# Bias of both attentions: from stages of its own into the attention stages

## The chip, the cores and the metric

The kernel runs on one core of a Trainium2 chip. The metric is the device time of one execution in microseconds (us). Three runs of the kernel before gave 3819.38, 3820.43 and 3822.8 us, median 3820.43 us.

## The reference

The model is a trunk of two layers over 1024 tokens of width 1024, each a mixer and a SwiGLU block. Layer 0 mixes with a gated recurrence (HGRN2) and with an attention of 8 heads over three dilated patterns, (window, dilation) = (128, 1), (512, 4), (2048, 16), whose three softmaxes are joined by their log sums. Layer 1 (NSA) has 16 query heads on 4 key heads and adds three attentions: over compressed blocks, over selected blocks, and over a window of 512.

The kernel folds the parts of the score that depend on the distance d = query - key alone into an additive bias. In layer 0 a key within reach of n patterns has weight n: the bias is log(n), or -1e30 where n = 0 or d < 0. In layer 1 there are two masks, each 0 or -1e30: causal (d >= 0) and window (0 <= d < 512).

## The kernel before

The program is a sequence of stages. Each opens its semaphores and buffers, gives every engine a list of instructions, and closes with a clearing of its semaphores and a barrier over all engines; nothing of a stage starts before that barrier (class `Stage`, line 56). Matmuls are done in split fp32: an operand is cut into a high part (ScalarE, `ACT.Copy`) and a low part (VectorE, subtract).

A bias is a table of 128 partitions x 1024 distances. It is used in two shapes: `rows` (as made) for the maxima of a query block, and `cols` (each 128x128 block transposed) for the scores. Both are added by matmuls against an identity.

Layer 0, between the recurrence and the attention, has two stages:
- `dilated_bias_stage` (line 2119): GpSimd's iota makes the distances (L2136); VectorE makes the bias in 15 instructions over 128x1024, each waiting for the one before (L2144 to L2164); GpSimd's affine_select puts -1e30 where d < 0 (L2138).
- `bias_parts_stage` (line 1292): 8 transposes on TensorE (L1305), `rows` and `cols` high by ScalarE (L1309, L1311), `cols` low by VectorE (L1317).

Layer 1, between the selection and the attention, has three: `distance_bias_stage` (line 2168: a memset and two affine_selects on GpSimd, L2176 to L2181), and `bias_parts_stage` for the causal and for the window mask, without a low part.

`attention_stage` (line 1341) is called twice, as "at0" with 2 heads a round and as "at1" with 4; both have 4 rounds over loops written out by hand. Its beginning sets the order around the change:
- GpSimd makes `base` (L1515, L1517, L1520);
- ScalarE copies the identity, and from `base` fills parts of `ka` and `kc` (L1625, four times L1631); VectorE clears constants and `qa` (L1678 to L1682). These count `setup` up to 7;
- SyncE waits for `setup` 7 and issues the loads of queries, keys and values (L1483, L1493, L1496);
- TensorE waits for `setup` 7 and for the first loads, and does the maxima of the first unit (L1550), on which everything else of the stage depends. VectorE takes the maxima from PSUM (L1686), GpSimd builds `shift` (L1529), TensorE does the scores (L1570), ScalarE the exponentials into `pr` (L1637).
- In later rounds SyncE reloads a head's queries when the head's last values are done (`pv_done`, L1509), and TensorE waits for them.

Of the kernel before, what the change touches and what calls it, by code (L numbers as in the profile page):

```python
# [17 lines left out]
F32 = mybir.dt.float32  # L18
# [6 lines left out]
P = 128  # L25
# [1263 lines left out]
                    tokens(n)  # L1289


def bias_parts_stage(nc, name, bias, rows, cols, ident):


    with Stage(nc, name) as st:
        tr = st.ps("tr", [P, 2, BANK])
        tr_done, hi_done = st.sem("tr_done"), st.sem("hi_done")
        block = st.block()
        hi, lo = cols

        @block.tensor
        def _(pe):
            for d in range(TT):
                at = SEQ - (d + 1) * P
                nc.tensor.transpose(tr[:, d // 4, (d % 4) * P:(d % 4 + 1) * P], bias[:, at:at + P], ident[:]).then_inc(tr_done, 1)  # L1305

        @block.scalar
        def _(act):
            nc.scalar.activation(rows[:], bias[:], ACT.Copy)  # L1309
            act.wait_ge(tr_done, TT)  # L1310
            nc.scalar.activation(hi[:], tr[:, :, :].rearrange("p a b -> p (a b)"), ACT.Copy).then_inc(hi_done, 1)  # L1311

        @block.vector
        def _(dve):
            if lo is not None:
                dve.wait_ge(hi_done, 1)
                nc.vector.tensor_tensor(lo[:], tr[:, :, :].rearrange("p a b -> p (a b)"), hi[:].bitcast(F32), ALU.subtract)  # L1317


class Branch:  # L1320


# [18 lines left out]
def attention_stage(nc, name, n_heads, qT, branches, mixed, col0, ident, gates=None, selT=None):  # L1341
# [47 lines left out]
    with Stage(nc, name) as st:  # L1389
# [11 lines left out]
        rl = st.sb("rl", [P, U, S])  # L1401
        sc = st.sb("sc", [P, U, S])
        o_sb = st.sb("o", [P, S, HD])
        ps_m = st.ps("ps_m", [P, 2, BANK])
        ps_s = st.ps("ps_s", [P, RB, BANK])
        ps_o = st.ps("ps_o", [V1, 2, BANK])
# [1 line left out]
        q_in = [st.sem(f"q_in{h}") for h in range(H)]  # L1408
        k_in = [st.sem(f"k_in{s}") for s in range(SETS)]
        v_in = [st.sem(f"v_in{s}") for s in range(SETS)]  # L1410
        block_row, setup, m_done, piece_done, top_done, shift_done, s_done, p_done, hi_done, lo_done, pv_done, v_hi_done = (
            st.sem(n) for n in ("block_row", "setup", "m_done", "piece_done", "top_done", "shift_done", "s_done", "p_done", "hi_done",
                                "lo_done", "pv_done", "v_hi_done"))
# [3 lines left out]

        maxima_at = {step: [] for step in range(-C, C)}
        for u in range(U):
# [89 lines left out]
        @block.gpsimd  # L1512
        def _(pool):

            nc.gpsimd.memset(base[:], 1.0).then_inc(block_row, 1)  # L1515
            pool.wait_ge(block_row, 1)
            nc.gpsimd.affine_select(out=base[:], in_=base[:], compare_op=ALU.is_ge, fill=0.0, base=SLC * SEL0,  # L1517
                                    pattern=[[1, SEQ]], channel_multiplier=-SLC).then_inc(block_row, 1)
            pool.wait_ge(block_row, 2)
            nc.gpsimd.affine_select(out=base[:], in_=base[:], compare_op=ALU.is_ge, fill=0.0, base=SLC - 1 - SLC * SEL0,  # L1520
                                    pattern=[[-1, SEQ]], channel_multiplier=SLC).then_inc(block_row, 1)
            ident4 = ident[:].rearrange("p (o c) -> p o c", o=1).to_broadcast([P, S, P])

            with pool.Fori(0, ROUNDS) as it:
                for u in range(U):

                    pool.wait_ge(top_done, it * U + u + 1)
                    pool.nop(nofuse=True)
                    nc.gpsimd.tensor_tensor(shift[:, u % 2, :].rearrange("p (n c) -> p n c", c=P), ident4,  # L1529
                                            bcast(top[:, u, 0, :].rearrange("p (n o) -> p n o", o=1), P), ALU.mult)\  # L1530
                        .then_inc(shift_done, 1)

        @block.tensor
        def _(pe):
            pe.wait_ge(setup, 7)
            def maxima(it, m):
                u, x, j, w, _ = pieces[m]
                s, hh, br, strip = units[u]
# [85 lines left out]
        def _(act):  # L1624
# [27 lines left out]
            def split(it, s):  # L1652
                act.wait_ge(v_in[s], it * 16 + 16)
                nc.scalar.activation(v_hi[:, s, :, 0:HD], v_raw[:, s, :, :], ACT.Copy).then_inc(v_hi_done, 1)

            split(0, 0)
            for c in range(3):
                exps(0, c)
# [18 lines left out]
        def _(dve):  # L1677
# [2 lines left out]
                nc.vector.memset(to[:, :, :, HD:V1].bitcast(F32), value)  # L1680
            nc.vector.memset(qa[HD:P, :, :].bitcast(F32), 0.0).then_inc(setup, 1)
            nc.vector.memset(o_sb[:], 0.0).then_inc(o_free, 1)  # L1682
            def maximum(it, m):
                u, x, _, w, half = pieces[m]
                dve.wait_ge(m_done, it * M + m + 1)
                ins = nc.vector.tensor_reduce(top[:, u, half, x:x + 1], ps_m[:, m % 2, 0:w * P], AX.X, ALU.max)  # L1686
                ins.then_inc(piece_done, 1)
                if m == pieces_of[u][-1]:
                    dve.wait_ge(piece_done, it * M + m + 1)
                    ins = nc.vector.tensor_tensor(top[:, u, 0, :], top[:, u, 0, :], top[:, u, half, :], ALU.max)  # L1690
                    ins.then_inc(top_done, 1)
# [424 lines left out]
            output(TT - 1)  # L2116


def dilated_bias_stage(nc, bias):

    reach = ((128, 1), (512, 4), (2048, 16))
    with Stage(nc, "dil") as st:
        d = st.sb("d", [P, SEQ], I32)
        r = st.sb("r", [P, SEQ], I32)
        df = st.sb("df", [P, SEQ])
        a = st.sb("a", [P, SEQ])
        b = st.sb("b", [P, SEQ])
        c = st.sb("c", [P, SEQ])  # L2130
        step, iota_done = st.sem("step"), st.sem("iota_done")
        block = st.block()

        @block.gpsimd
        def _(pool):
            nc.gpsimd.iota(d[:], pattern=[[-1, SEQ]], base=SEQ - P, channel_multiplier=1).then_inc(iota_done, 1)  # L2136
            pool.wait_ge(step, 15)
            nc.gpsimd.affine_select(out=bias[:], in_=a[:], compare_op=ALU.is_ge, fill=NEG, base=SEQ - P,  # L2138
                                    pattern=[[-1, SEQ]], channel_multiplier=1)

        @block.vector
        def _(dve):
            dve.wait_ge(iota_done, 1)
            nc.vector.tensor_copy(df[:], d[:]).then_inc(step, 1)  # L2144
            dve.wait_ge(step, 1)
            nc.vector.tensor_scalar(c[:], df[:], float(reach[0][0]), None, ALU.is_le).then_inc(step, 1)
            for n, (window, dilation) in enumerate(reach[1:]):

                at = 2 + 4 * n
                nc.vector.tensor_scalar(r[:], d[:], dilation - 1, None, ALU.bitwise_and).then_inc(step, 1)  # L2150
                dve.wait_ge(step, at + 1)
                nc.vector.tensor_scalar(a[:], r[:], 0.0, None, ALU.is_equal).then_inc(step, 1)
                dve.wait_ge(step, at + 2)
                nc.vector.scalar_tensor_tensor(b[:], df[:], float(window), a[:], ALU.is_le, ALU.mult).then_inc(step, 1)
                dve.wait_ge(step, at + 3)
                nc.vector.tensor_tensor(c[:], c[:], b[:], ALU.add).then_inc(step, 1)
                dve.wait_ge(step, at + 4)

            nc.vector.tensor_scalar(a[:], c[:], 0.0, NEG, ALU.is_equal, ALU.mult).then_inc(step, 1)
            for n, count in enumerate((2, 3)):  # L2160
                at = 11 + 2 * n
                nc.vector.tensor_scalar(b[:], c[:], float(count), math.log(count), ALU.is_equal, ALU.mult).then_inc(step, 1)
                dve.wait_ge(step, at + 1)
                nc.vector.tensor_tensor(a[:], a[:], b[:], ALU.add).then_inc(step, 1)  # L2164
                dve.wait_ge(step, at + 2)


def distance_bias_stage(nc, causal, window):

    with Stage(nc, "dist") as st:  # L2170
        step = st.sem("step")
        block = st.block()

        @block.gpsimd
        def _(pool):
            nc.gpsimd.memset(causal[:], 0.0).then_inc(step, 1)  # L2176
            pool.wait_ge(step, 1)
            nc.gpsimd.affine_select(out=causal[:], in_=causal[:], compare_op=ALU.is_ge, fill=NEG, base=SEQ - P,
                                    pattern=[[-1, SEQ]], channel_multiplier=1).then_inc(step, 1)
            pool.wait_ge(step, 2)  # L2180
            nc.gpsimd.affine_select(out=window[:], in_=causal[:], compare_op=ALU.is_ge, fill=NEG, base=WIN - 1 - (SEQ - P),  # L2181
                                    pattern=[[1, SEQ]], channel_multiplier=-1)


def store_stage(nc, x_sb, out):
    with Stage(nc, "store") as st:
        x_out = st.sem("x_out")
# [8 lines left out]
def trunk(nc, x, attn_norm, ffn_norm, hy_w_in, hy_lb_logits, hy_o_gain, hy_q_gain, hy_k_gain, hy_w_out, nsa_w_in,  # L2196
# [22 lines left out]
    with ExitStack() as whole:  # L2219
        def sb(ctx, name, shape, dt=F32):  # L2220
            return ctx.enter_context(nc.sbuf_tensor(name, shape, dt))
# [26 lines left out]
        with ExitStack() as c:  # L2248
            mixed = sb(c, "mixed0", [P, TT, DM])
            hgrn_stage(nc, proj0, hy_lb_logits, mixed, ident)  # L2250
            with ExitStack() as c2:
                rows, cols = sb(c2, "dil_rows", [P, SEQ], F32R), parts(c2, "dil_cols", [P, SEQ])
                with ExitStack() as c3:
                    bias = sb(c3, "dil_bias", [P, SEQ])
                    dilated_bias_stage(nc, bias)
                    bias_parts_stage(nc, "dil_parts", bias, rows, cols, ident)
                at = 4 * A_WIDTH + 2 * B_HEADS * HD
                dilated = Branch(k0T, proj0[:, at:at + B_HEADS * HD], 1, rows, cols, range(TT), TT)
                attention_stage(nc, "at0", B_HEADS, q0T, [dilated], mixed, A_WIDTH, ident)
# [22 lines left out]
        with ExitStack() as c:  # L2282
            mixed = sb(c, "mixed1", [P, TT, DM])
            with ExitStack() as c2:
# [4 lines left out]
                masks = []  # L2289
                for mask in ("causal", "window"):  # L2290
                    masks.append((sb(c2, f"{mask}_rows", [P, SEQ], F32R), [sb(c2, f"{mask}_cols", [P, SEQ], F32R), None]))
                with ExitStack() as c3:
                    causal, window = sb(c3, "causal", [P, SEQ]), sb(c3, "window", [P, SEQ])
                    distance_bias_stage(nc, causal, window)
                    bias_parts_stage(nc, "causal_parts", causal, *masks[0], ident)
                    bias_parts_stage(nc, "window_parts", window, *masks[1], ident)
                vs, vw = DM + 3 * KV_W, DM + 5 * KV_W
                picked = Branch(some(k1T, 0), proj1[:, vs:vs + KV_W], GROUP, *masks[0], (0,), TT, C_HEADS, True)
                near = Branch(some(k1T, 4), proj1[:, vw:vw + KV_W], GROUP, *masks[1], (0, WIN // P), WIN // P + 1, 2 * C_HEADS)
# [27 lines left out]
```

## Time and profile before

| | |
|---|---|
| median of 3 runs | 3820.43 us |
| the profiled execution, its own time | 3820.43 us |
| its span, first to last instruction | 3818.7 us |
| TensorE busy | 3304.1 us (87%) |
| VectorE, ScalarE, GpSimd busy | 43%, 32%, 4% |
| mean granted TensorE clock | 0.926 |

The profile is one execution. A busy share is a mean over stages; the change touches two short stretches between long stages, so what counts is how long each stretch is and which instruction ends it. PE is TensorE, PEld its weight load, DVE VectorE, ACT ScalarE, POOL GpSimd, SP SyncE; a q behind the name is the engine's queue. PEclk 1.00 is 2.4 GHz, 0.50 is 1.2 GHz.

### The profile page before, as it was taken

Reading aid. Unit: us, or ns where it says so; the run is one execution under the profiler, and the core shown is the slowest. Engines: PE = TensorE matmul, PEld = TensorE weight load, DVE = VectorE, ACT = ScalarE, POOL = GpSimd, SP = SyncE. Lnnn points to the kernel's source line nnn. Section 1 sums busy time; section 2 is a strip of 40 time slices with the busy share of each in tenths; the row PEclk is TensorE's granted clock in tenths of the full one; section 3 lists DMA queues with packets and bytes.
Section 4 is the critical chain, followed back from the end, with each engine's and each line's share of the span. In section 5 each row is a group of like instructions: output and inputs, shape, how many; then the busy total and the mean of one; then the engine's idle time right before and its main releaser. Section 6 shows DMA issues by size and latency. Waiting matters only on the chain. (4 is left out here: it accounts for less than half of the span.)

```text
span 3818.7 us, 44633 instructions
## 1 busy us (share of the span) xinstructions
PE 3304.1 (87%) x16522; PEld 2764.2 (72%) x16522; DVE 1623.4 (43%) x2983; ACT 1204.1 (32%) x2469; POOL 149.1 (4%) x189
## 2 busy tenths in 40 slices
PE   5999575578779999999799755999998889999998
PEld 4887465466658888888588654877877768888887
DVE  3132776445332323232442054887887133232323
ACT  3122332334122112212332153665665122121211
POOL 0000000000000000000000121111110000000000
PEclk9999687789889999999899676999999989999999
DMA  3334100332111212121273513113111022212212
GB/s 119 97 101 105 38 19 23 68 68 45 47 44 54 79 45 83 55 72 50 64 171 93 102 37 68 33 34 67 34 33 35 16 61 64 67 61 69 69 53 88
DMA packets 264014, 241.70 MB, mean 63 GB/s; under 512 B 41944, under 2 KB 203736, under 8 KB 263800
## 3 DMA queue, kind: packets, MB, share of 16 engines
q1 hardware_dynamic: 263800, 238.86, 23.7%
q8 instruction: 133, 2.18, 0.2%
q14 instruction: 81, 0.66, 0.1%
HBM read 193.52 MB, written 45.29 MB: 63 GB/s over the span
## 5 line engine op out<-in xcount | busy, mean ns | idle before, releaser
L498 PE MATMUL ffn_acc<-ffn_hT_hi,ffn_w_hi 128*128 128x512 f32 x1408 | 435.8, 391 | 17.8 <-DVE ffn_w_lo L579 17.8
L498 PE MATMUL ffn_acc<-ffn_hT_lo,ffn_w_hi 128*128 128x512 f32 x1408 | 435.4, 391 | 0.0
L498 PE MATMUL ffn_acc<-ffn_hT_hi,ffn_w_lo 128*128 128x512 f32 x1408 | 435.2, 390 | 0.0
L579 DVE TENSOR_TENSOR ffn_w_lo<-ffn_raw,ffn_w_hi 128x1024 fp32r<-128x1024 f32 x88 | 107.8, 1225 | 738.8 <-ACT ffn_w_hi L538 738.8
L1153 PE MATMUL in_acc<-in_w_hi,hT_hi 128*128 128x512 f32 (+1 forms) x832 | 330.4, 397 | 15.2 <-DVE in_w_lo L1233 15.2
L538 ACT ACTIVATE ffn_w_hi<-ffn_raw 128x1024 fp32r<-128x1024 f32 x88 | 93.3, 1060 | 750.4 <-PE ffn_acc L498 737.4
L1637 ACT ACTIVATE at_pr<-at_ps_s 128x512 f32<-128x512 f32 x480 | 223.8, 466 | 332.6 <-PE at_ps_s L1570 330.1
L1155 PE MATMUL in_acc<-in_w_hi,hT_lo 128*128 128x512 f32 (+1 forms) x832 | 325.1, 391 | 0.0
L1154 PE MATMUL in_acc<-in_w_lo,hT_hi 128*128 128x512 f32 (+1 forms) x832 | 324.7, 390 | 0.0
L1696 DVE TENSOR_TENSOR at_p_lo<-at_pr,at_p_hi 128x512 fp32r<-128x512 f32 x480 | 272.6, 585 | 108.9 <-ACT at_p_hi L1644 108.5
L498 PEld LDWEIGHTS ffn_acc<-ffn_hT_hi,ffn_w_hi 128*128 128x128 f32 x1408 | 265.5, 189 | 73.4 <-DVE ffn_w_lo L579 18.3
L498 PEld LDWEIGHTS ffn_acc<-ffn_hT_lo,ffn_w_hi 128*128 128x128 f32 x1408 | 265.5, 189 | 55.3
L498 PEld LDWEIGHTS ffn_acc<-ffn_hT_hi,ffn_w_lo 128*128 128x128 f32 x1408 | 265.5, 189 | 55.3
L1686 DVE TENSOR_REDUCE at_top<-at_ps_m 128x1 f32<-128x512 f32 (+1 forms) x480 | 243.4, 525 | 128.4 <-PE at_ps_m L1550 125.7
L518 PE MATMUL ffn_acc_d<-ffn_d_hi,ffn_a_hi 128*128 128x512 f32 x704 | 274.0, 389 | 0.0
L520 PE MATMUL ffn_acc_d<-ffn_d_hi,ffn_a_lo 128*128 128x512 f32 x704 | 274.0, 389 | 0.0
L519 PE MATMUL ffn_acc_d<-ffn_d_lo,ffn_a_hi 128*128 128x512 f32 x704 | 274.0, 389 | 0.0
L1550 PE MATMUL at_ps_m<-at_kc,at_qa 128*128 128x512 f32 (+1 forms) x480 | 177.2, 382 | 106.6 <-DMA at_qb<-q0T_lo 36.5
L1644 ACT ACTIVATE at_p_hi<-at_pr 128x512 fp32r<-128x512 f32 x480 | 237.9, 497 | 0.0
L1153 PEld LDWEIGHTS in_acc<-in_w_hi,hT_hi 128*128 128x128 f32 x832 | 165.1, 198 | 46.4 <-DVE in_w_lo L1233 17.5
L549 ACT ACTIVATE ffn_d_hi<-ffn_d_raw 128x512 fp32r<-128x512 f32 x176 | 108.3, 629 | 277.9 <-PE ffn_acc_d L520 277.9
L1550 PEld LDWEIGHTS at_ps_m<-at_kc,at_qa 128*128 128x128 f32 x480 | 95.1, 198 | 138.2 <-issue 78.5
(310 smaller groups left out, 5779.3 us busy)
## 6 DMA issues: line engine op xcount, KB each, us to landing
ffn_d_raw<-in_ffn_w_down SPq DMA_DIRECT2D x176, 256.0 KB, 3.0
ffn_raw<-in_ffn_w_gate SPq DMA_DIRECT2D x44, 512.0 KB
ffn_raw<-in_ffn_w_up SPq DMA_DIRECT2D x44, 512.0 KB
in_raw<-in_hy_w_in SPq DMA_DIRECT2D x56, 256.0 KB
proj<-in_nat SPq DMA_DIRECT2D x40, 256.0 KB, 2.1
in_raw<-in_nsa_w_in SPq DMA_DIRECT2D x40, 256.0 KB
at_qa<-q1T_hi SPq DMA_DIRECT2D x16, 264.0 KB
x_sb<-in_x SPq DMA_DIRECT2D x1, 4096.0 KB
```

The lines of the kernel that those rows point to most:

```text
L498: ins = nc.tensor.matmul(acc[:, m, half, :], w[:, m, k, :], h[:, k, half * HALF:(half + 1) * HALF], start=k == 0 and w is w_hi and h is hT ...
L518: nc.tensor.matmul(acc_d[:, x, :], a_hi[:, k, rows], d_hi[:, n % R, :], start=k == 0, stop=False)
L519: nc.tensor.matmul(acc_d[:, x, :], a_hi[:, k, rows], d_lo[:, n % R, :], start=False, stop=False)
L520: ins = nc.tensor.matmul(acc_d[:, x, :], a_lo[:, k, rows], d_hi[:, n % R, :], start=False, stop=k == G - 1)
L1153: nc.tensor.matmul(acc[:, n % 4, 0:cols], x_hi, r_hi, start=k == 0, stop=False)
L1154: nc.tensor.matmul(acc[:, n % 4, 0:cols], x_hi, r_lo, start=False, stop=False)
L1155: ins = nc.tensor.matmul(acc[:, n % 4, 0:cols], x_lo, r_hi, start=False, stop=k == KD - 1)
L1550: ins = nc.tensor.matmul(ps_m[:, m % 2, pos * P:(pos + n) * P], lhsT, rhs, start=x == 0, stop=x == len(parts) - 1, skip_group_check=True)
L1637: nc.scalar.activation(pr[:, c % R, 0:w], ps_s[:, c % RB, 0:w], ACT.Exp).then_inc(p_done, 1)
L1644: nc.scalar.activation(p_hi[:, c % R, 0:w], pr[:, c % R, 0:w], ACT.Copy).then_inc(hi_done, 1)
L1686: ins = nc.vector.tensor_reduce(top[:, u, half, x:x + 1], ps_m[:, m % 2, 0:w * P], AX.X, ALU.max)
L1696: nc.vector.tensor_tensor(p_lo[:, c % R, 0:w], pr[:, c % R, 0:w], p_hi[:, c % R, 0:w].bitcast(F32), ALU.subtract).then_inc(lo_done, 1)
```

## The change

The five stages go. What they did stands at the beginning of `attention_stage`. The table being made lies in `pr` (`temp(n)`, two of its six buffers each), the transposes go to banks of `ps_s` and `ps_m`; only the dilated chain has a new buffer, `more`, of 3 x 1024 a partition. GpSimd does its part behind `base`, VectorE its 15 instructions behind its memsets, ScalarE its copies behind the four L1631 and ahead of the first values' split. TensorE does the transposes ahead of its wait for `setup`, and begins the maxima only when the `cols` are done.

```diff
-def bias_parts_stage(nc, name, bias, rows, cols, ident):
...
@@ attention_stage
+        dilated = gates is None
+        more = st.sb("more", [P, 3, SEQ]) if dilated else None
...
+        def temp(n):
+            return pr[:, 2 * n:2 * n + 2, :].rearrange("p a b -> p (a b)")
+
+        bias_tr_of = [ps_s[:, 0:2, :].rearrange("p a b -> p (a b)"), ps_m[:].rearrange("p a b -> p (a b)")]
+        NBIAS = 1 if dilated else 2
...
@@ gpsimd, behind base
+            if dilated:
+                nc.gpsimd.iota(temp(1).bitcast(I32), pattern=[[-1, SEQ]], base=SEQ - P, channel_multiplier=1).then_inc(iota_done, 1)
+                pool.wait_ge(bias_step, 15)
+                nc.gpsimd.affine_select(out=temp(0), in_=more[:, 0, :], compare_op=ALU.is_ge, fill=NEG, base=SEQ - P,
+                                        pattern=[[-1, SEQ]], channel_multiplier=1).then_inc(bias_done, 1)
+            else:
+                nc.gpsimd.memset(temp(0), 0.0).then_inc(bias_step, 1)
+                pool.wait_ge(bias_step, 1)
+                nc.gpsimd.affine_select(out=temp(0), in_=temp(0), compare_op=ALU.is_ge, fill=NEG, base=SEQ - P,
+                                        pattern=[[-1, SEQ]], channel_multiplier=1).then_inc(bias_done, 1)
+                pool.wait_ge(bias_done, 1)
+                nc.gpsimd.affine_select(out=temp(1), in_=temp(0), compare_op=ALU.is_ge, fill=NEG, base=WIN - 1 - (SEQ - P),
+                                        pattern=[[1, SEQ]], channel_multiplier=-1).then_inc(bias_done, 1)
...
@@ tensor
+            for n in range(NBIAS):
+                pe.wait_ge(bias_done, n + 1)
+                for d in range(TT):
+                    at = SEQ - (d + 1) * P
+                    ins = nc.tensor.transpose(bias_tr_of[n][:, d * P:(d + 1) * P], temp(n)[:, at:at + P], ident[:])
+                ins.then_inc(bias_tr, 1)
             pe.wait_ge(setup, 7)
+            pe.wait_ge(cols_done, NBIAS)
...
@@ scalar, behind setup
+            for n in range(NBIAS):
+                act.wait_ge(bias_done, n + 1)
+                nc.scalar.activation(branches[n].rows[:], temp(n), ACT.Copy)
+                act.wait_ge(bias_tr, n + 1)
+                nc.scalar.activation(branches[n].cols[0][:], bias_tr_of[n], ACT.Copy).then_inc(cols_hi if dilated else cols_done, 1)
             split(0, 0)
...
@@ vector, behind the memsets; the 15 instructions of dilated_bias_stage, in buffers of pr and more
+            if dilated:
+                d, df, a, b, c, r = (temp(1).bitcast(I32), temp(2), more[:, 0, :], more[:, 1, :], more[:, 2, :], more[:, 1, :].bitcast(I32))
+                dve.wait_ge(iota_done, 1)
...
+                dve.wait_ge(cols_hi, 1)
+                nc.vector.tensor_tensor(branches[0].cols[1][:], bias_tr_of[0], branches[0].cols[0][:].bitcast(F32), ALU.subtract)\
+                    .then_inc(cols_done, 1)
...
@@ trunk
-                with ExitStack() as c3:
-                    bias = sb(c3, "dil_bias", [P, SEQ])
-                    dilated_bias_stage(nc, bias)
-                    bias_parts_stage(nc, "dil_parts", bias, rows, cols, ident)
...
-                    distance_bias_stage(nc, causal, window)
-                    bias_parts_stage(nc, "causal_parts", causal, *masks[0], ident)
-                    bias_parts_stage(nc, "window_parts", window, *masks[1], ident)
```

## Rows read from the trace of the kernel before

**Rows 1.** Page, part 1: busy us (share) xinstructions.

```profile
PE 3304.1 (87%) x16522; PEld 2764.2 (72%) x16522; DVE 1623.4 (43%) x2983; ACT 1204.1 (32%) x2469; POOL 149.1 (4%) x189
```

**Rows 2.** Windows view of the stretches: from:to, length, busy by engine.

```profile
core 0: us, PE busy (x) PEld busy (x) DVE busy (x) ACT busy (x) POOL busy (x), PEclk, DMA share, GB/s
664.03:685.70 21.67, 1.94 (x8) 1.57 (x8) 14.63 (x16) 2.08 (x2) 2.02 (x3) 0.50 0.00 0
685.70:707.11 21.41, 0.00 (x0) 0.00 (x0) 2.27 (x5) 4.20 (x5) 3.03 (x3) 0.50 0.65 113
707.11:716.30 9.19, 8.85 (x24) 6.33 (x24) 4.13 (x9) 2.51 (x3) 1.04 (x1) 0.50 0.94 163
2315.38:2327.03 11.65, 3.88 (x16) 3.14 (x16) 0.00 (x0) 4.16 (x4) 3.02 (x3) 0.50 0.00 0
2327.03:2349.18 22.15, 0.00 (x0) 0.00 (x0) 3.97 (x5) 4.20 (x5) 3.03 (x3) 0.50 0.66 114
...
707.11:960.00 252.89, 199.07 (x1024) 160.45 (x1024) 124.26 (x248) 99.79 (x217) 20.12 (x17) 0.90 0.30 60
2349.18:2930.00 580.82, 554.49 (x3581) 467.19 (x3582) 474.28 (x1092) 351.57 (x840) 72.29 (x64) 0.99 0.19 39
```

**Rows 3.** Timeline, layer 0's two bias stages: start, length, what, [idle before].

```profile
658.90 4.42 DVE L1032 TENSOR_TENSOR mixed<-mixed,hgo_sg 128x4096 f32<-128x4096 f32 x1
664.03 0.98 POOL L2136 IOTA dil_d<- 128x1024 int32 x1 [281.29 <-ACTq L67]
665.05 0.69 DVE L2144 CAST dil_df<-dil_d 128x1024 f32<-128x1024 int32 x1 [1.72 <-POOL dil_d L2136]
...
677.64 1.23 DVE L2164 TENSOR_TENSOR dil_a<-dil_a,dil_b 128x1024 f32<-128x1024 f32 x1
679.01 1.04 POOL L2138 TENSOR_SCALAR_AFFINE_SELECT dil_bias<-dil_a 128x1024 f32<-128x1024 f32 x1 [14.00 <-DVE dil_a L2164]
...
680.76 1.06 ACT L1309 ACTIVATE dil_rows<-dil_bias 128x1024 fp32r<-128x1024 f32 x1 [29.53 <-PEq L70]
680.79 1.94 PE L1305 MATMUL dil_parts_tr<-ident,dil_bias 128*128 128x128 f32 x8 [43.31 <-PEq L70]
682.76 1.02 ACT L1311 ACTIVATE dil_cols_hi<-dil_parts_tr 128x1024 fp32r<-128x1024 f32 x1 [0.94 <-PE dil_parts_tr L1305]
683.82 1.22 DVE L1317 TENSOR_TENSOR dil_cols_lo<-dil_parts_tr,dil_cols_hi 128x1024 fp32r<-128x1024 f32 x1 [4.95 <-ACT dil_cols_hi L1311]
```

**Rows 4.** Timeline, the beginning of at0.

```profile
685.70 0.95 POOL L1515 MEMSET at_base<- 128x1024 f32 x1 [5.65 <-POOLq L70]
...
686.72 1.04 POOL L1517 TENSOR_SCALAR_AFFINE_SELECT at_base<-at_base 128x1024 f32<-128x1024 f32 x1
687.83 1.04 POOL L1520 TENSOR_SCALAR_AFFINE_SELECT at_base<-at_base 128x1024 f32<-128x1024 f32 x1
688.38 0.27 DVE L1682 MEMSET at_o<- 128x256 f32 x1
...
691.75 1.04 ACT L1631 ACTIVATE at_kc<-at_base 64x1024 fp32r<-64x1024 f32 x1
692.81 0.38 SPq L1483 DMA_DIRECT2D at_qa<-q0T_hi  x1
...
707.14 0.45 PE L1550 MATMUL at_ps_m<-at_kc,at_qa 128*128 128x128 f32 x1 [24.42 <-DMA at_kb<-k0T_hi]
```

**Rows 5.** Timeline, layer 1: the mask stages and the beginning of at1.

```profile
2315.38 0.95 POOL L2176 MEMSET causal<- 128x1024 f32 x1 [41.12 <-POOLq L70]
...
2333.08 1.04 ACT L1631 ACTIVATE at_kc<-at_base 64x1024 fp32r<-64x1024 f32 x1
...
2349.22 0.45 PE L1550 MATMUL at_ps_m<-at_kc,at_qa 128*128 128x128 f32 x1 [24.14 <-DMA at_kb<-k1T_hi]
```

**Rows 6.** Waits view of 707 to 1010 us: us in total, times, longest.

```profile
PE at_ps_m L1550 <- DMA at_qb<-q0T_lo: 36.5, 6, 6.8
```

**Rows 7.** Page, part 5: a VectorE instruction that runs while weights stream in.

```profile
L579 DVE TENSOR_TENSOR ffn_w_lo<-ffn_raw,ffn_w_hi 128x1024 fp32r<-128x1024 f32 x88 | 107.8, 1225 | 738.8 <-ACT ffn_w_hi L538 738.8
```

More of the change, by code:

```diff
@@ L1289, in _ @@
                     tokens(n)
-def bias_parts_stage(nc, name, bias, rows, cols, ident):
[L1295 to L1317, printed above, removed]
 class Branch:
@@ L1410, in attention_stage @@
         v_in = [st.sem(f"v_in{s}") for s in range(SETS)]
+        bias_step, bias_done, bias_tr, cols_hi, cols_done, iota_done = (
+            st.sem(n) for n in ("bias_step", "bias_done", "bias_tr", "cols_hi", "cols_done", "iota_done"))
         block_row, setup, m_done, piece_done, top_done, shift_done, s_done, p_done, hi_done, lo_done, pv_done, v_hi_done = (
@@ L1415, in attention_stage @@
         block = st.block()
+        def temp(n):
+            return pr[:, 2 * n:2 * n + 2, :].rearrange("p a b -> p (a b)")
+        bias_tr_of = [ps_s[:, 0:2, :].rearrange("p a b -> p (a b)"), ps_m[:].rearrange("p a b -> p (a b)")]
+        NBIAS = 1 if dilated else 2
+        reach = ((128, 1), (512, 4), (2048, 16))
         maxima_at = {step: [] for step in range(-C, C)}
@@ L1682, in _ @@
             nc.vector.memset(o_sb[:], 0.0).then_inc(o_free, 1)
+            if dilated:
+                d, df, a, b, c, r = (temp(1).bitcast(I32), temp(2), more[:, 0, :], more[:, 1, :], more[:, 2, :], more[:, 1, :].bitcast(I32))
+                dve.wait_ge(iota_done, 1)
+                nc.vector.tensor_copy(df, d).then_inc(bias_step, 1)
+                dve.wait_ge(bias_step, 1)
+                nc.vector.tensor_scalar(c, df, float(reach[0][0]), None, ALU.is_le).then_inc(bias_step, 1)
+                for n, (reached, dilation) in enumerate(reach[1:]):
+                    at = 2 + 4 * n
+                    nc.vector.tensor_scalar(r, d, dilation - 1, None, ALU.bitwise_and).then_inc(bias_step, 1)
+                    dve.wait_ge(bias_step, at + 1)
+                    nc.vector.tensor_scalar(a, r, 0.0, None, ALU.is_equal).then_inc(bias_step, 1)
+                    dve.wait_ge(bias_step, at + 2)
+                    nc.vector.scalar_tensor_tensor(b, df, float(reached), a, ALU.is_le, ALU.mult).then_inc(bias_step, 1)
+                    dve.wait_ge(bias_step, at + 3)
+                    nc.vector.tensor_tensor(c, c, b, ALU.add).then_inc(bias_step, 1)
+                    dve.wait_ge(bias_step, at + 4)
+                nc.vector.tensor_scalar(a, c, 0.0, NEG, ALU.is_equal, ALU.mult).then_inc(bias_step, 1)
+                for n, count in enumerate((2, 3)):
+                    at = 11 + 2 * n
+                    nc.vector.tensor_scalar(b, c, float(count), math.log(count), ALU.is_equal, ALU.mult).then_inc(bias_step, 1)
+                    dve.wait_ge(bias_step, at + 1)
+                    nc.vector.tensor_tensor(a, a, b, ALU.add).then_inc(bias_step, 1)
+                    dve.wait_ge(bias_step, at + 2)
+                dve.wait_ge(cols_hi, 1)
+                nc.vector.tensor_tensor(branches[0].cols[1][:], bias_tr_of[0], branches[0].cols[0][:].bitcast(F32), ALU.subtract)\
+                    .then_inc(cols_done, 1)
             def maximum(it, m):
@@ L2116, in _ @@
             output(TT - 1)
[L2119 to L2165, printed above, removed]
@@ L2168, in distance_bias_stage @@
[L2168 to L2182, printed above, removed]
@@ L2291, in trunk @@
                     masks.append((sb(c2, f"{mask}_rows", [P, SEQ], F32R), [sb(c2, f"{mask}_cols", [P, SEQ], F32R), None]))
-                with ExitStack() as c3:
-                    causal, window = sb(c3, "causal", [P, SEQ]), sb(c3, "window", [P, SEQ])
-                    distance_bias_stage(nc, causal, window)
-                    bias_parts_stage(nc, "causal_parts", causal, *masks[0], ident)
-                    bias_parts_stage(nc, "window_parts", window, *masks[1], ident)
                 vs, vw = DM + 3 * KV_W, DM + 5 * KV_W
```

## The prediction

> **What bounds the kernel now.** The page's first part says that TensorE is busy for 87% of the span [rows 1]. That share says little here: the change lies in the other 13%. So I read windows next, one for each stretch between the last work of the stage ahead and the first maxima of the attention. There are four of them, and in all four TensorE stands nearly still. The two bias stages of layer 0 take 21.67 us, with 14.63 us of VectorE as the longest term; the three of layer 1 take 11.65 us; the beginnings of at0 and at1 take 21.41 and 22.15 us, with no TensorE work, 2.3 to 4.2 us on each other engine and a DMA share of 0.65 [rows 2]. The timeline says what ends each: in the bias stages, the chain of instructions itself and the barriers; in the beginnings, the loads. TensorE's first maxima come at 707.14 and at 2349.22 us and both were released by the DMA of `kb` [rows 4, 5]. The reader is to see two serial pieces, one made of engine work and one made of transfers, on disjoint resources: in the bias stages the DMA share is 0.00.
>
> **What is removed.** The stretches 664.03 to 685.70 and 2315.38 to 2327.03, barriers included: 21.67 + 11.65 = 33.32 us [rows 2]. Both begin with the first instruction behind the barrier of the stage ahead (the last VectorE work there ends at 658.90 + 4.42 = 663.32, 0.71 us earlier) [rows 3], and end with the first instruction of the attention stage, so the attention stage will begin where they began. Its own 0.7 us of barrier stays.
>
> **What the beginning of at0 becomes.** I count from its first instruction, T0 (685.70 before).
> - Loads: GpSimd's `base` ends at 687.83 + 1.04 = T0 + 3.17; ScalarE's last fill at 691.75 + 1.04 = T0 + 7.09; the first load is issued at T0 + 7.11 [rows 4]. The diff puts nothing ahead of any of them: GpSimd's new work is behind `base`, ScalarE's behind the fills, VectorE's behind the memset that counts for `setup`, and nothing is added on SyncE. The loads land as before, and TensorE could start at 707.14 - 685.70 = T0 + 21.44.
> - The bias chain, link by link: iota behind `base`, with the 0.07 us gap between instructions of GpSimd [rows 4] and 0.98 us: T0 + 4.22. VectorE has by then ended its memsets (688.38 + 0.27 = T0 + 2.95) [rows 4] and starts 0.04 us later; its 15 instructions took from 665.05 to 677.64 + 1.23 = 678.87, 13.82 us: T0 + 18.08. The select starts 0.14 us later and takes 1.04: T0 + 19.26. Transposes, 0.07 + 1.94: T0 + 21.27. The high part, 0.03 + 1.02: T0 + 22.32. The low part, 0.04 + 1.22: T0 + 23.58. TensorE's wait, 0.07 [rows 3].
> - So TensorE starts at T0 + 23.65 instead of T0 + 21.44: the wait for `cols_done` now ends last, not the loads. The slip is 2.2 us.
>
> What is queued behind that wait is all of TensorE's list, and through it VectorE's maxima, GpSimd's `shift` and the exponentials. Does the slip reach the end of the stage? The other head's loads are in by then either way, and would hide it if TensorE met them late; but the waits for loads that follow (six, 36.5 us in all) [rows 6] are for reloads that SyncE issues only when TensorE has finished a head. They move with TensorE and absorb nothing. I take the slip in full; its ends are 0 and 7 us (the rivals below). Gain of layer 0: 21.67 - 2.2 = 19.5 us.
>
> **What the beginning of at1 becomes.** No VectorE chain here. GpSimd: `base` to T0 + 3.17 as in at0, then a memset and two selects, 0.95 + 1.04 + 1.04 with gaps of at most 0.14: T0 + 6.6. ScalarE is free at 2333.08 + 1.04 = 2334.12, T0 + 7.09 (T0 = 2327.03) [rows 2, 5], and then has two copies of 1.06 and two of 1.02 us [rows 3]: T0 + 11.3. The 16 transposes, from T0 + 5.5 on, lie beside it. TensorE can't start before the loads, at 2349.22 = T0 + 22.19 [rows 5], so 10.9 us of cover stay. The masks cost nothing and the gain is all of 11.65 us. If the cover were gone, it would cost what goes beyond those 10.9 us.
>
> **Costed at nothing.** The instructions in their new place beside loads: a VectorE instruction of 128x1024 with two inputs takes 1.225 us where weights stream in [rows 7], and 1.22 us in the bias stage with no DMA at all [rows 3]; so loads don't stretch it. Six more semaphores to clear at each end of attention, and the buffer `more`: no row prices them; the barrier with all around it is 0.71 us [rows 3], so I bound them by 0 and 0.7 us a stage and take 0, since they add no instruction to a chain.
>
> **The clock.** The clock was at 0.50 over the bias stages and the beginnings, and for 9.19 us after the first maxima of at0, in which TensorE was busy for 8.85 us [rows 2]. Now 1.94 us of transposes end 2.4 us before the first maxima; before, 24 us before. If they brought the rise forward by their own length and the gap, 4.3 us of the 9.19 would run at the double clock, and where TensorE's own work bounds them that gives back up to 4.3 / 2 = 2.2 us. I take 0, because eight transposes alone left the clock at 0.50 in both bias stretches. The Trainium skill, TensorE: Matmul & The Clock Gate, "The HAM clock gate", says that the half rate is the default and activity releases it, by which the result would be about 2 us lower, 3787; its part "PE-mode transpose" says that transposes don't count as such activity, by which it stays at 3789.
>
> **Sum.** 19.5 + 11.65 = 31.1 us. The profiled execution took 3820.43 us over a span of 3818.7, and equals the median of the runs. Predicted: 3820.43 - 31.1 = 3789.3 us.
>
> **The rivals.**
> - *The slip isn't passed on* (an earlier rise of the clock as above, or something later in the round that is late anyway). For it: nearly all of the 9.19 us is TensorE work at the low clock [rows 2]. Against it: the reloads follow TensorE [rows 6]. Gain 33.3 us: 3787.1 us.
> - *The chain is longer in its new place.* Nine of its 15 instructions have one input and take 0.69 us, six have two and take 1.22 [rows 3]; if the nine lost what makes them short (buffers cut out of `pr` and `more`, ScalarE's fills and the loads beside them), each would cost 0.53 more, 4.8 us, all of it on the path: a slip of 7 us, 3794.1 us. Against it: loads don't stretch the two-input kind [rows 7], and every buffer is still 1024 adjacent elements.
> - *The gaps that are removed come back elsewhere* (the attention stage needs time of its own to get going, which the bias stages had covered, so that the loads' issue comes later than T0 + 7.11). Were it so in both layers by as much as the barrier gap is long, 0.7 us each, nothing is seen; to cancel the gain to within 0.2% it would need 23 of 31 us. No row shows such a cost. About 3815 us.
> - *Slower: the clock.* The two attentions run at 0.90 and 0.99 from the first maxima on [rows 2], that is about 50 and 12 us at the low level. At that level a stretch bound by TensorE takes twice its time. If the new phase of the six reload waits and of the start made the clock rise later each time, this would have to add more than 62 us at the low level to lose 31 us: from there on the kernel is slower. With a doubling of both, and then some 16 us more beyond the level where it breaks even, the time is 3828 us. Against it: the waits stay as long as they were and TensorE's lists are the same.
>
> **How the numbers follow.** Forecast 0.76, its own range 3787 to 3792; not passed on 0.10; longer chain 0.09; gaps back 0.02; clock 0.01; the last 0.02 for a case I don't see, shared between no change and slower. The range reaches to the first two rivals and takes in 0.7 us a stage of the unpriced clearing, plus 1.7 us, half the spread of the runs before: 3785 to 3796. A measurement of this kernel tells some 0.2% (7.6 us) from no change. Faster by more: 0.76 + 0.10 + 0.09 = 0.95; within: 0.03; slower: 0.02.
>
> **What would show it.** In the profile after: at0's first GpSimd memset at 664.0 and its first load 7.1 us later; VectorE's chain 13.8 us long; the first maxima at 664.0 + 23.65 = 687.7, with ScalarE's or VectorE's `cols` as the releaser of TensorE's wait instead of `kb`. For at1: T0 at 2295.9, `cols` done at T0 + 11.3, first maxima at T0 + 22.2 = 2318.1, released by the DMA as before. The stretch from the first maxima of at0 to T0 of at1 (2315.38 - 707.14 = 1608.2 us) is unchanged. Wrong would be: loads issued later than T0 + 7.2; a chain over 14.5 us; a first maximum of at1 that waits for `cols_done`; or a changed length between the maxima of at0 and those of at1 by more than 2 us, which would mean that clock or slip work on later.

## The result and the profile after

| | before | after |
|---|---|---|
| median of 6 runs each | 3820.75 us | 3792.38 us |
| lowest to highest | 3816.77 to 3826.38 | 3788.32 to 3794.28 |
| profiled execution, its own time / span | 3820.43 / 3818.7 us | 3790.27 / 3788.6 us |
| mean granted clock | 0.926 | 0.932 |

The ratio is 0.9923 (95% interval 0.991 to 0.9936): 28.4 us less by the medians, 24 to 34 by the interval. The forecast was 31.1 us less, 3789.3 us; the interval holds it.

The windows of the kernel after, as in [rows 2]: the beginning of at0, the time at the low clock after its first maxima, at0's body (first maxima to last values), and the beginning of at1.

```profile
661.15:684.82 23.67, 1.97 (x9) 1.60 (x9) 16.91 (x21) 7.32 (x9) 5.01 (x5) 0.50 0.69 118
684.82:693.19 8.37, 8.07 (x22) 5.89 (x23) 3.71 (x8) 1.14 (x2) 1.04 (x1) 0.50 0.87 167
684.82:933.95 249.13, 201.20 (x1019) 162.09 (x1020) 123.97 (x246) 98.15 (x215) 19.16 (x16) 0.89 0.29 58
2295.70:2316.87 21.17, 3.54 (x17) 3.31 (x17) 3.98 (x5) 8.02 (x9) 6.00 (x6) 0.58 0.64 112
```

The reader is to see that VectorE's chain of 14.6 us and the loads (DMA share 0.69) now lie in one stretch of 23.67 us, where there were two, of 21.67 and 21.41 us [rows 2]. The timeline gives the links of the chain, to be laid beside [rows 3, 4]:

```profile
661.15 0.95 POOL L1498 MEMSET at_base<- 128x1024 f32 x1 [278.14 <-POOLq L70]
...
664.28 0.98 POOL L1506 IOTA at_pr<- 128x1024 int32 x1
665.29 0.69 DVE L1695 CAST at_pr<-at_pr 128x1024 f32<-128x1024 int32 x1 [1.20 <-POOL at_pr L1506]
...
668.26 0.38 SPq L1466 DMA_DIRECT2D at_qa<-q0T_hi  x1
...
677.89 1.23 DVE L1713 TENSOR_TENSOR at_more<-at_more 128x1024 f32<-128x1024 f32 x1
679.26 1.04 POOL L1508 TENSOR_SCALAR_AFFINE_SELECT at_pr<-at_more 128x1024 f32<-128x1024 f32 x1 [14.01 <-DVE at_more L1713]
680.34 1.06 ACT L1662 ACTIVATE dil_rows<-at_pr 128x1024 fp32r<-128x1024 f32 x1 [12.10 <-POOL at_pr L1508]
680.36 1.97 PE L1535 MATMUL at_ps_s<-ident,at_pr 128*128 128x128 f32 x8 [45.79 <-POOL at_pr L1508]
682.36 1.02 ACT L1664 ACTIVATE dil_cols_hi<-at_ps_s 128x1024 fp32r<-128x1024 f32 x1 [0.97 <-PE at_ps_s L1535]
683.49 1.22 DVE L1716 TENSOR_TENSOR dil_cols_lo<-at_ps_s,dil_cols_hi 128x1024 fp32r<-128x1024 f32 x1 [4.38 <-ACT dil_cols_hi L1664]
...
684.82 0.45 PE L1554 MATMUL at_ps_m<-at_kc,at_qa 128*128 128x128 f32 x1 [2.49 <-issue]
```

The low part ends at 684.71 and the first maxima start at 684.82; the row no longer names the DMA. In e1, where the beginning of at0 is the same, the row names the low part:

```profile
688.89 0.44 PE L1654 MATMUL at_ps_m<-at_kc,at_qa 128*128 128x128 f32 x1 [2.50 <-DVE dil_cols_lo L1816]
```

at1's first maxima are still released by the DMA, 10.2 us behind the end of the last `cols` (2305.62 + 1.01 = 2306.63):

```profile
2305.62 1.01 ACT L1664 ACTIVATE window_cols<-at_ps_m 128x1024 fp32r<-128x1024 f32 x1
...
2316.87 0.44 PE L1554 MATMUL at_ps_m<-at_kc,at_qa 128*128 128x128 f32 x1 [12.32 <-DMA at_kb<-k1T_hi]
```

Where the 30.1 us between the two spans lie (four of the six stretches aren't changed):

| stretch | before | after | difference |
|---|---|---|---|
| start to the first instruction behind the recurrence | 664.03 | 661.15 | -2.9 |
| from there to at0's first maxima | 43.11 | 23.67 | -19.4 |
| at0's body | 246.87 | 249.13 | +2.3 |
| its end to the first instruction behind the selection | 1361.37 | 1361.75 | +0.4 |
| from there to at1's first maxima | 33.84 | 21.17 | -12.7 |
| to the end | 1469.5 | 1471.7 | +2.2 |

The -2.9 us come ahead of anything that the change touches, and they are luck: over the kernels of this document this stretch takes 661.2 to 665.2 us. In the two profiles here the clock goes with it: over 382 to 433 us, in the recurrence, it is at 0.50 in the profile before and rises 6 us earlier in the one after:

```profile
382.00:433.00 51.00, 13.22 (x60) 12.45 (x61) 36.16 (x50) 17.72 (x15) 0.75 (x3) 0.50 0.24 63
```

```profile
382.00:433.00 51.00, 12.86 (x82) 11.90 (x83) 37.19 (x53) 17.72 (x15) 1.01 (x4) 0.56 0.25 64
```

### The profile page after: what moved, and what is told of

It reads as the page before. It is cut to its first block and busy times, and to the rows that moved or that the text cites. A ratio compares the mean times of both kernels' runs of the same rounds, so it can differ in the third digit from the quotient of the medians.

```text
span 3788.6 us, 44515 instructions
## 1 busy us (share of the span) xinstructions
PE 3305.4 (87%) x16522; PEld 2764.5 (73%) x16522; DVE 1624.0 (43%) x2983; ACT 1204.2 (32%) x2469; POOL 148.6 (4%) x189
## 5 line engine op out<-in xcount | busy, mean ns | idle before, releaser
L1155 PEld LDWEIGHTS in_acc<-in_w_hi,hT_lo 128*128 128x128 f32 x832 | 165.0, 198 | 31.1
```

What stands on the lines that cost most here:

```text
L1155: ins = nc.tensor.matmul(acc[:, n % 4, 0:cols], x_lo, r_hi, start=False, stop=k == KD - 1)
```

## The experiments

Every kernel but e12 was built from the kernel after by the edit shown. Ratios are taken against runs of the kernel before on the same chip (medians 3819.1 us beside e1 to e4, 3820.7 beside e5 to e8, 3820.0 beside e9 to e11). Where a time is compared with the kernel after (3792.38 us), the two weren't run beside each other, and from chip to chip the kernel before alone differs by 1.6 us; four or five runs of one kernel spread over 3 to 9 us. Such differences are good to some 3 us.

**e1: only layer 0.** `attention_stage` skips its own making in at1, and `trunk` calls the old stages there.

> Only layer 0's bias is made inside its attention stage; layer 1 keeps its three stages. Theory (the removed stretch less a slip of 2.2 us at the first maxima, rest unchanged): 19.5 us under before, some 3801 us; at0's first maxima at T0 + 23.65, at1's at T0 + 22.2 or, as in the changed kernel, 21.2. Rival (nothing of the slip is passed on): 21.7 us under before. Second rival (gains of the two layers are not additive, one of them covers the other): well off 19.5.

3802.52 us, ratio 0.9954 (0.9937 to 0.997): 17 us less, interval 11 to 24. First maxima at T0 + 23.68. The interval holds both 19.5 and 21.7, so it doesn't decide between theory and rival (e3 does); the profile places the slip where theory has it. at0's body was 250.1 us.

**e2: only layer 1.** The reverse.

> Only layer 1's masks are made inside its attention stage; layer 0 keeps its two stages. Theory (the removed stretch in full, all new work under the loads): 11.7 us under before, 12.7 if the loads land 1 us earlier after T0 as in the changed kernel; at1's first maxima released by the DMA of kb at T0 + 21.2 to 22.2. Rival (the gain of the changed kernel comes from layer 0 alone): no change.

3808.99 us, ratio 0.9973 (0.9964 to 0.9983): 10 us less, interval 6 to 14. at1's first maxima at T0 + 21.3, released by the DMA. The rival falls. The two parts add to 27 us, against 28 for the whole.

**e3: a longer chain in at0.**

```diff
+                for n in range(8):
+                    nc.vector.tensor_tensor(c, c, c, ALU.max).then_inc(chain_more, 1)
+                    dve.wait_ge(chain_more, n + 1)
                 nc.vector.tensor_scalar(a, c, 0.0, NEG, ALU.is_equal, ALU.mult).then_inc(bias_step, 1)
```

> The changed kernel with eight more VectorE instructions of 128x1024 in at0's bias chain (a maximum of c with itself, 1.22 us and a gap of 0.04 each). Theory (the chain ends last and its length goes to the end of the kernel one to one): 8 x 1.26 = 10.1 us over the changed kernel, first maxima at T0 + 33.8. Rival (the slip is taken up by something later in the first round, the reloads or the clock): under 6 us.

3802.14 us, 9.8 us over the changed kernel, for 10.1 us of chain; first maxima at T0 + 33.75. The body behind them takes 249.1 us, as in the kernel after, so nothing there took the delay up: what the chain adds goes to the end.

**e4: a longer mask in at1.**

```diff
                 pool.wait_ge(bias_done, 1)
+                for n in range(20):
+                    nc.gpsimd.affine_select(out=temp(1), in_=temp(0), ...).then_inc(chain_more, 1)
+                    pool.wait_ge(chain_more, n + 1)
```

> The changed kernel with twenty more affine_selects of 128x1024 ahead of the window mask in at1 (1.04 us and a gap of 0.14 each, 23.6 us). Theory (masks have 9.9 us of cover under the loads, from cols done at T0 + 11.3 to the first maxima at T0 + 21.2): the window mask comes at T0 + 30, cols at T0 + 33.2, first maxima there too and released by cols_done: 12 us over the changed kernel, not 23.6. Rival (masks were on the path already): 23.6 us over it. Second rival (other work than the loads covers more): under 8 us.

3803.86 us, 11.5 us over the changed kernel, for 23.5 us of selects. Timeline of at1's beginning (T0 = 2298.86):

```profile
2298.86 0.95 POOL L1499 MEMSET at_base<- 128x1024 f32 x1 [41.48 <-POOLq L70]
...
2304.25 23.49 POOL L1518 TENSOR_SCALAR_AFFINE_SELECT at_pr<-at_pr 128x1024 f32<-128x1024 f32 x20
...
2330.99 1.02 ACT L1669 ACTIVATE window_cols<-at_ps_m 128x1024 fp32r<-128x1024 f32 x1 [0.97 <-PE at_ps_m L1540]
...
2332.11 0.45 PE L1559 MATMUL at_ps_m<-at_kc,at_qa 128*128 128x128 f32 x1 [1.16 <-issue]
```

First maxima at T0 + 33.25, right behind the `cols`, and 12.1 us later than in the kernel after. Of the 23.6 us that the selects put in front of the window mask, 10.2 went into the cover under the loads (10.9 were worked out, 9.9 expected here), and 1.4 into the time in which ScalarE had been busy with other copies; the rest was paid. So the masks are made under the loads, and the cover is about as large as worked out.

**e5 and e6: the chain of at0 by one instruction shorter or longer.**

```diff
-                    nc.vector.scalar_tensor_tensor(b, df, float(reached), a, ALU.is_le, ALU.mult).then_inc(bias_step, 1)
+                    if reached < SEQ: (the line above) else: nc.vector.nop(nofuse=True).then_inc(bias_step, 1)
...
-                    nc.vector.tensor_tensor(c, c, b, ALU.add).then_inc(bias_step, 1)
+                    nc.vector.tensor_tensor(c, c, b if reached < SEQ else a, ALU.add).then_inc(bias_step, 1)
```

e6 adds one of e3's eight instructions.

> The changed kernel without the reach test of the third pattern in at0's chain (2048 reaches every distance, the bias is the same): 1.22 us and its gap less. Theory (the chain ends last, and the TensorE clock's level after each wait for loads hangs on where the waits fall): first maxima at T0 + 22.4; the clock is low for 9.6 us after them, as in the kernel before, and low for 3 to 4 us, not 5 to 6, after the first reload; at0's body, first maxima to last values, back from 249.1 to 250.1 us to the 245 to 247 us it had with the bias outside; 2 to 4 us under the changed kernel. Rival (only the chain counts): body 249 us and 1.3 us under the changed kernel.

> The changed kernel with one more VectorE instruction (maximum of c with itself) in at0's chain, 1.26 us. Theory of the clock: first maxima at T0 + 24.9, low clock for some 7.1 us after them instead of 8.4, and 3.6 to 4.4 us after the first reload instead of 4.9 to 5.7, body shorter by 1 us or more; the kernel as fast as the changed one or faster in spite of the longer chain. Rival: body unchanged and 1.3 us over the changed kernel.

3792.35 and 3792.67 us, with the changed kernel at 3792.38. First maxima at T0 + 22.52 and T0 + 24.92. The clock was low for 9.6 us after the first maxima in e5, as said; in e6 it rose after 3.7 us, not 7.1. After the first reload it was low for 6.2 us in e5 (3 to 4 expected) and 5.4 in e6 (3.6 to 4.4 expected). The bodies were 248.4 and 249.4 us: shorter than 249.1 to 250.1 by at most 1.7 us, not back at 245 to 247. As I had put it, my theory of the body fails. A chain of 1.2 us more or less can't be told in the total either, so neither rival (1.3 us less, 1.3 us more) is settled by the times.

**What the body is made of.** So I took the body apart in every profile: the gaps of TensorE at the six reloads (over 4 us from one matmul's start to the next's; in e9 and e11, described below, the matmuls thrown away don't count), the time outside them at a granted clock of 0.50, and the rest. Half of the low time is what it would cost if TensorE alone bounded it.

| profile | body | gaps | low clock | body - gaps - low/2 |
|---|---|---|---|---|
| before | 246.9 | 37.8 | 34.4 | 191.9 |
| before, once more (e12) | 244.1 | 35.1 | 32.2 | 192.8 |
| e2 (layer 0 as before) | 244.9 | 35.5 | 35.1 | 191.8 |
| after | 249.1 | 37.2 | 40.1 | 191.9 |
| e1 | 250.1 | 38.4 | 39.7 | 191.9 |
| e3 | 249.1 | 38.2 | 37.8 | 192.0 |
| e4 | 249.0 | 37.9 | 38.1 | 192.1 |
| e5 | 248.4 | 38.3 | 36.8 | 191.7 |
| e6 | 249.4 | 40.1 | 33.2 | 192.7 |
| e7 | 252.6 | 40.8 | 39.8 | 191.9 |
| e8 | 248.0 | 37.8 | 37.0 | 191.7 |
| e10 | 247.3 | 38.4 | 30.9 | 193.5 |
| e9 (reload fill) | 234.2 | 36.7 | 8.5 | 193.3 |
| e11 (reload fill) | 236.2 | 39.8 | 3.4 | 194.6 |

The last column lies within 1.1 us (191.7 to 192.8) wherever the low time is 32 us or more: the body holds no new work (1019 matmuls before and after), it differs by waits for reloads and by clock. With less low time the column rises, to 194.6 us in e11: half of the low time overstates what the clock costs, by up to 3 us of 18 here. And with the bias outside the body is 244.1 to 246.9 us in three profiles, with the bias inside and the reloads unfilled 247.3 to 252.6 in nine.

**e7, e8, e10: idle time of TensorE ahead of the first maxima filled.** e7 and e10 with transposes, e8 with fp32r matmuls of 128 columns:

```diff
+            def filler(n):
+                for _ in range(n):
+                    nc.tensor.transpose(ps_t[:, 0, 384:512], ident[:], ident[:])
+            if dilated:
+                pe.wait_ge(setup, 7)
+                filler(45)
             for n in range(NBIAS):
...
             pe.wait_ge(setup, 7)
+            filler(8 if dilated else 48)
```

> The changed kernel with idle time of TensorE ahead of the first maxima filled with transposes of the identity into unused columns of ps_t: in at0 45 ahead of the bias and 8 behind it, in at1 48 behind the bias (0.246 us each at the low clock, from the bias transposes of the trace). If transposes don't raise the granted clock: it stays at 0.50 until 8.4 us after the first maxima, no change in time. Rival (any TensorE work raises it): 1.00 before the first maxima of both attentions, up to 4 us less in at0 and up to 5 us less in at1.

> The same with fp32r matmuls of the identity with itself, 128 columns (0.107 us each at the low clock by the start to start of the 128-column rows): in at0 110 ahead of the bias and 20 behind it, in at1 120. Theory (matmuls raise the clock, and the 8.4 and 11.4 us at the low clock after the first maxima are bound by TensorE only in part): clock 1.00 at the first maxima of both, 2 to 4 us less in each, 4 to 8 us under the changed kernel. Rival (the ramp is hidden behind VectorE's maxima): under 2 us.

> As e7, with as many transposes as it takes to leave TensorE no gap up to the first maxima: in at0 85 ahead of the bias and 18 behind it, in at1 105 behind it. e7 had the clock up during the transposes and down again after 4 to 5 us of idling. Theory: clock 1.00 at both first maxima; the 8.4 us at the low clock after at0's and 11.2 us after at1's go, 4 us less in at0 and, because VectorE's maxima bound the beginning of at1, 1 to 4 us there: 5 to 8 us under the changed kernel. Rival (what e7's time of 3798 us suggests: filling costs time or gains none): as the changed kernel or slower.

e7: 3798.22 us, 5.8 over the changed kernel, where no change or a gain was expected; e8: 3806.20, 13.8 over it, where 4 to 8 less were expected; e10: 3791.92 (ratio 0.9925, 0.9909 to 0.9942), where 5 to 8 less were expected. In windows of e10, the first transposes in at0, the rest with the bias, the time after the first maxima, and a stretch of at1:

```profile
670.10:674.30 4.20, 4.18 (x20) 4.18 (x21) 4.06 (x5) 0.00 (x0) 0.00 (x0) 0.50 0.61 163
674.30:685.70 11.40, 10.40 (x93) 9.93 (x91) 7.70 (x8) 2.08 (x2) 1.04 (x1) 1.00 1.12 175
685.73:694.10 8.37, 7.68 (x34) 5.40 (x35) 5.34 (x12) 3.01 (x4) 1.04 (x1) 1.00 0.88 168
2323.00:2333.20 10.20, 9.26 (x30) 7.69 (x30) 5.37 (x13) 2.18 (x5) 2.08 (x2) 0.50 0.98 182
```

Transposes alone brought the clock to 1.00. In e7 they had too, at 675.9, but TensorE then stood still from 679 to 683.6 us, the clock fell, and the first maxima were at 0.50 again. The fills don't explain why e7 is slower: its first maxima are at T0 + 23.62, but its profile has the longest body of all, 3.6 us of it longer gaps. In e8 the matmuls take 0.213 us from start to start, twice what I had read, so at0's first maxima came 12.9 us late, which is most of the 13.8; and through 29 us of them (with the eight transposes of the bias in between) the clock stayed at 0.50, of which this is a part:

```profile
676.00:682.00 6.00, 6.00 (x30) 6.00 (x30) 5.50 (x6) 0.00 (x0) 0.21 (x1) 0.50 1.09 184
```

With the clock up at its start, e10 gained nothing that can be measured. In at0 the first maxima came 0.9 us earlier and the body was 247.3 us, within the scatter of the rest. In at1 the clock was at 1.00 at the first maxima (2320.74), but fell at 2323.0 and stayed at 0.50 for 10.2 us (last row above): the low time there was put off, not saved.

**e9: the reload waits filled.** The 22 matmuls run ahead of the wait for a reloaded head; for that, TensorE's wait for a free bank was moved ahead of both.

```diff
+                        for _ in range(22):
+                            nc.tensor.matmul(ps_m[:, m % 2, :], ident_r[:], branches[0].rows[:, 0:BANK],
+                                             start=True, stop=True, skip_group_check=True)
                     pe.wait_ge(q_in[hh], (it + 1) * (16 * n_q))
```

> The changed kernel with 22 matmuls of 512 columns (0.216 us each at the high clock, 4.8 us) on TensorE ahead of each of at0's six waits for reloads, into the bank that the next maxima overwrite. Theory (at0's body is 191.9 us, plus the gaps of TensorE, plus half of the time that it works at the low clock, 33 to 40 us in ten profiles): the clock stays at 1.00 over the waits, some 30 us at the low clock go, body 249 less 15 = 234 us, 12 to 15 us under the changed kernel; the gaps, measured from the last real work, stay 5 to 7.5 us. Rival (the waits are as long as they are, so the low clock behind them is hidden): no change.

3778.66 us, ratio 0.9893 (0.9876 to 0.9909), 13.7 us under the changed kernel. Window of the body, to be laid beside that of the kernel after, which shows 249.13 us and 0.89:

```profile
686.37:920.60 234.23, 217.81 (x1152) 174.75 (x1152) 123.49 (x246) 98.71 (x216) 19.19 (x16) 0.98 0.31 62
```

Low clock 8.5 us instead of 40; gaps 36.7 us instead of 37.2. The body was expected at 234 us and came at 234.2: the edit changed one term of the table, and the body followed. The rival falls.

**e11: all together.** e5 + e9 + e10.

> Everything together: the shorter chain of e5, the reload fill of e9, the transposes of e10 (14 instead of 18 behind at0's bias). If the gains add: 17 to 24 us under the changed kernel, 3769 to 3776 us. If the low clock is hidden behind waits: as the changed kernel.

3774.40 us (3767.98 to 3776.63), ratio 0.9874 (0.9857 to 0.989): the fastest here, 18 us under the changed kernel and 46 under before, at the slow end of what was expected. The single gains add to 14 us (e9 13.7, e10 0.5, e5 none); the rest isn't told from scatter. First maxima at T0 + 22.1, body 236.2 us at a clock of 0.99, 2 us longer than e9's in spite of the higher clock: its gaps are 3.1 us longer.

**e12: the kernel before once more.**

> The kernel before, unchanged, for a second look at two stretches that the one profile of it shows: at0's body (first maxima to last values), 246.9 us there, 244.9 us with the same layer 0 in e2, and 247.3 to 252.6 us in every profile with the bias inside and no reload fill; and the time from at1's beginning to its first maxima, 22.2 us there, 21.0 to 21.3 in e1 and e2. If the body is longer because of the change: 245 to 247 us again. If it is chance, how the waits fall on the clock's changes: anything up to 250. If the first maxima of at1 vary by chance: 21 to 22 us.

Span 3819.1 us; body 244.1 us; at1's first maxima at T0 + 22.2. The body is even under the 245 to 247 us expected: that points to the change, not to chance, though with three profiles against nine. The 22.2 us of at1 came again as well, but with 21.0 in e1 (masks outside) and 20.9 to 22.1 with them inside they don't go by where the masks are made. The clock was low for only 3.5 us after at0's first maxima, where the first profile of the same kernel had over 9.

## Why the prediction was right, and where it was off

- *What is removed, 33.3 us, barriers included.* Right: the attention stage begins 0.7 us behind the last VectorE work of the stage ahead (656.03 + 4.43 = 660.46, then 661.15), and loads issue at T0 + 7.11, as before. The rival of gaps that come back falls.
- *The chain of at0, T0 + 23.65.* Measured T0 + 23.67, and 23.6 to 23.7 in e1, e4, e7 and e9. VectorE's chain took 13.83 us (forecast 13.82). Part of the 0.02 us is luck: VectorE started 0.1 us earlier than I had added up, and the last two links took 0.1 us more. The rival of a longer chain falls: instructions of 0.69 us took 0.69 beside loads and ScalarE. What the loads alone would have allowed is less sharp than T0 + 21.44: T0 + 20.6 in e12 and 21.2 in e2, so the slip is 2.2 to 3.1 us.
- *The slip is passed on.* Right (e3: 9.8 us for 10.1, where the rival had under 6). The rival falls.
- *at1 hides all of it, with 10.9 us of cover.* Right in kind and size (e4). The masks gained 12.7 us by the profile instead of 11.65, because the first maxima came at T0 + 21.2, not 22.2; a load time scatters by about 1 us between profiles.
- *"The stretch from the first maxima of at0 to T0 of at1 is unchanged."* Wrong by 2.6 us in the profile (1610.9 for 1608.2), beyond the 2 us that I had allowed. The term was taken as nothing and is at0's body: 3.9 us more with the bias inside (mean 249.2 of the six profiles without any fill, 245.3 of the three with the bias outside), 2.2 of it longer gaps at the reloads and 1.9 half of the longer low clock. By the profiles this, less the 1 us that at1's loads gave, is what is missing between 31.1 and 28.4 us; the times alone can't show it, since their interval holds 31.1, and stretches that nothing touches moved by more. The clock rival named the place, the six waits, and in small it happened; its slower case didn't.
- *Why the gaps are longer is open.* The reloads are the same transfers in the same order. From the first issue of a reload to the end of the fourth it takes 2.25 us with the bias outside and 2.40 inside, from there to TensorE's next matmul 7.51 and 7.84 us (means of the same nine profiles): most of the growth is in the transfers, not in SyncE's issuing, and single profiles overlap. e5 and e6 show that moving the start by 1.2 us doesn't bring the old body back. Code and buffers lie elsewhere in memory; that wasn't tried.
- *The clock at at0's start.* I had taken 0 for it, because eight transposes alone left it at 0.50. Low for 8.4 us instead of over 9.2 [rows 2]: the 0 isn't contradicted, but it isn't tested by this either, since the kernel before itself had 3.5 us in e12 and e3 to e6 had 3.7 to 9.6. The reason was too weak, as more transposes do raise the clock: 4.2 us of them in e10, and in the kernel after itself the sixteen of at1, back to back from 2301.0 to 2304.6 us, behind which it was at 1.00 from 2304.3 to 2307.7 (hence the 0.58 of the fourth window); in e5 the same sixteen left it at 0.50. The Trainium skill, TensorE: Matmul & The Clock Gate, "PE-mode transpose", says that the full clock doesn't engage for transposes; e10's trace disagrees, with 1.00 over 11.4 us of them. Its part "The HAM clock gate" says that activity releases the half rate: so it was with these transposes, but 29 us of e8's 128-column matmuls didn't release it.
- *The range.* Its upper end, 3796 us, is less than the terms named for it add to (3794.1 + 1.4 + 1.7 = 3797.2). The result doesn't come near it.

## What to carry to other kernels

Stages that are serial for want of order, not of resources, can be laid over each other: write down the chain of each from the common start, link by link from the trace, and the longer one is the new length, to 0.1 us here. Then look for what the removed time doesn't explain where TensorE waits repeatedly: a body is its work plus its gaps plus nearly half of the time at the low clock, and keeping TensorE busy through short waits gave half as much again as the whole change.

## What the runs showed that I had not expected

- Six waits of 5 to 7 us at the reloads cost not 37 us but some 52: the low clock behind them cost about 15 more (body 249.1 us, 234.2 in e9), and 22 matmuls thrown away at each gave it back.
- Back-to-back fp32r matmuls of 128 columns, each with its weight load, ran at 0.213 us for 29 us without raising the clock (e8, at0). In at1 sixteen transposes went ahead of them; the clock rose 2 us into the same matmuls, at 2320.6, and the rest ran at 0.11 us and a clock of 1.00.
- Parts of the kernel which no edit touches moved by 4 to 5 us between profiles: the stretch ahead of at0 (661.2 to 665.2 us), that from at0's body to at1 (1361.4 to 1365.6 us, less the 11.65 us of masks where these stand in it), and that behind at1's first maxima (1467.6 to 1472.4 us).
